# A ring of thirteen parts for gathered rows, walked in steps of two parts in place of five

## The chip, the cores and the metric

The kernel runs on one core of a Trainium2 chip, from one launch. The metric is the device time of the program in microseconds (us); lower is better. The unchanged kernel was run three times: 1429.01, 1425.98 and 1428.95 us, median 1428.95. Its engines are PE (TensorE), DVE (VectorE), ACT (ScalarE), POOL (GpSimd) and SP (SyncE); each works through its own instructions in program order and they meet by semaphores.

## What is computed

One decoder layer over 512 tokens of width 1024, all float32. A mixing part (causal stick-breaking attention with 8 heads of 64, beside a chunked gMLP, and one output projection) gives x1 by a layer norm. Then comes the part that takes most of the time, a retrieval of experts by product keys, cut from the reference:

```
q = (x @ w_q).reshape(B, S, 8, 2, 128)                  # 8 retrieval heads
scores = einsum('bshpk,hpnk->bshpn', q, sub_keys)       # two halves, 128 keys each
s1, i1 = top_k(scores[..., 0, :], 16);  s2, i2 = top_k(scores[..., 1, :], 16)
top_s, top_c = top_k(s1[..., :, None] + s2[..., None, :], 16)
ids = i1[top_c // 16] * 128 + i2[top_c % 16]            # 16 experts for each token and head
gates = softmax(top_s)
h   = einsum('thkd,td->thk', u_tab[ids], x)             # a dot with a row of u for each expert
act = gates * gelu(h)
out = einsum('thk,thkd->td', act, v_tab[ids])           # a weighted sum of the rows of v
```

So for each of 512 tokens, 8 heads and 16 experts a row of u (4 KB) and a row of v (4 KB) are needed. Afterwards a layer norm, a sigmoid gate with a per-layer embedding and a last layer norm follow.

## The kernel before, in words

**Units and rows.** Tokens lie on the 128 partitions, in four tiles. A unit is one tile with one head; there are 32 (`UNITS`), numbered from 0 in the order in which they are worked. A unit has 16 columns c, one for each chosen expert, and a column is one *row* here: one indirect DMA that brings, for each of the 128 tokens, the 8 KB row of the joined table `uv` (1024 floats of u, then 1024 of v), 1 MiB in all. The rows are numbered k = 16 u + c, 0 to 511.

**What is done with a row.** POOL issues the gather (L652). DVE forms the dot of its u half with x1 (L1813, a multiply with a running sum, written back into the same place; a short instruction then reads the sum into `hid`). ACT takes the gelu of a pair of columns at once (L1429), multiplies by the gates (L1432) and scales the v halves of both rows in place (L1439). PE adds each scaled row into PSUM by eight 128x128 transposes (L1181, `combine`), which count `slot_free` up by one for a row.

**The ring.** The rows live in `ring`, the first 14 x 1024 floats of each partition of `arena`: thirteen parts of 1024 floats and one spare behind, so that a row that begins at part 12 has room. A row takes two neighbouring parts, u half and v half. Row k begins at part (3 + 5k) mod 13. So the part of its u half is next written as the v half of row k + 5, and that of its v half as the u half of row k + 8. This is what the two waits ahead of each gather say: row k waits for the dot of row k - 5 (L646, `dots_done`, `U_LIFE`) and for the sum of row k - 8 (L648, `slot_free`, `V_LIFE`). The landings of the rows are told by eight semaphores `rows_in` in turn, and DVE waits for the one of its row (L1811).

```
part = (FIRST_PART + U_LIFE * (u * TOPK + c)) % PARTS
return ring[:, part * D:(part + 2) * D]
```

**The order of the work.** It is written out by hand. POOL has nothing but the gathers from 73 us on: a unit's gathers wait besides for its `ids`. DVE's stream is two dots, then a piece of other work, and so on: the ranking of the next unit's keys (`rank_keys`, `rank_sums`, `rank_rest`, `rank_ids`), the norms and other pieces of the tiles that are behind (`background`), and `add_run`, which takes a finished sum from PSUM. ACT has a pair of columns, then its background work, and once in each unit, at the column pair 5, the exponentials of the next unit's gates between two loads of function tables (L1477, L1485). PE has the transposes of each row; after those of column 10 the 32 matmuls of `query(u + 2)` (L866), after those of column 12 the four of `key_scores(u + 2)` (L878), and after each odd column a step of background matmuls (the projections of the other tiles, attention, output and gate products). Four queries stand elsewhere (`EARLY`). SP issues the weight loads.

```
for c in range(TOPK):
    combine(u, c)
    if c == 10 and u + 2 < NU and u + 2 not in EARLY:
        query(u + 2)
    if c == 12 and u + 2 < NU:
        key_scores(u + 2)
```

**The start and the end.** Before the gathers the ring holds other things: `w_out0` in parts 0 to 7, `e_0`, `l_0`, `pre_T` and `pre_q` in parts 8 and 9, and the first weights `w_gv` of the gv projection in parts 10, 11 and half of 12. Therefore two gathers of unit 0 wait for these projections (`gv_halves`, L642 and L644): column 4, which begins at part 10, and column 7, at part 12. In the last unit the columns from 11 on are gathered without the last quarter of their v half, two of them without any of it, and these pieces follow in seven gathers after row 511 (L660, L666).

Of the kernel before, what the change touches and what calls it, by code (L numbers as in the profile page):

```python
# [24 lines left out]
PH, TOPK, NKEY = 8, 16, 128  # L25
# [6 lines left out]
MASKED = -float(2 ** 30)  # L32
SEED = 1597463007.0

U_LIFE, V_LIFE = 5, 8
PARTS = U_LIFE + V_LIFE
FIRST_PART = 3
GRP = 2
OUT_PIECES = ((0, 512), (512, 832), (832, 1024))
LAST_COLS = (0, 288, 576, 864, D)  # L40
# [143 lines left out]
def build(nc, a, out):  # L184
    ctx = ExitStack()
    with ctx:
# [3 lines left out]
        def sem(name):  # L190
            return ctx.enter_context(nc.semaphore(name))
# [70 lines left out]

        def row(u, c):

            part = (FIRST_PART + U_LIFE * (u * TOPK + c)) % PARTS
            return ring[:, part * D:(part + 2) * D]

        late_sum = row(NU - 1, LATE)[:, PART:2 * D]
        y_1 = row(NU - 1, LATE)[:, 0:HALF]


# [109 lines left out]
        gv_halves = sem("gv_halves")  # L381
# [51 lines left out]
        rows_in = [sem(f"rows_in{i}") for i in range(V_LIFE)]  # L433
# [172 lines left out]
        @block.gpsimd  # L606
        def _(pool):
            nc.gpsimd.memset(ident[:, :], 0.0).then_inc(const_ready, 1)
            nc.gpsimd.memset(neg_tri[:, :], -1.0).then_inc(const_ready, 1)
            nc.gpsimd.memset(neg_one[:, :], -1.0).then_inc(const_ready, 1)  # L610
            nc.gpsimd.memset(neg_mask[:, :], MASKED).then_inc(const_ready, 1)
            nc.gpsimd.memset(ones[:, :], 1.0).then_inc(const_ready, 1)
            nc.gpsimd.iota(iota16[:, :], pattern=[[1, TOPK]], base=0, channel_multiplier=0,
                           allow_small_or_imprecise_dtypes=True).then_inc(const_ready, 1)
            pool.wait_ge(const_ready, 6)
            nc.gpsimd.affine_select(out=ident[:, :], in_=ident[:, :], compare_op=ALU.not_equal, fill=1.0,
                                    base=0, pattern=[[-1, P]], channel_multiplier=1).then_inc(const_ready, 1)
            nc.gpsimd.affine_select(out=neg_tri[:, :], in_=neg_tri[:, :], compare_op=ALU.is_ge, fill=0.0,
                                    base=0, pattern=[[-1, P]], channel_multiplier=1).then_inc(const_ready, 1)
            nc.gpsimd.affine_select(out=neg_mask[:, :], in_=neg_mask[:, :], compare_op=ALU.is_ge, fill=0.0,  # L620
                                    base=0, pattern=[[-1, P]], channel_multiplier=1).then_inc(const_ready, 1)
            pool.wait_ge(ws_in, 16)
            nc.gpsimd.affine_select(out=wsT, in_=wsT, compare_op=ALU.is_ge, fill=0.0, base=0,
                                    pattern=[[0, G], [1, P]], channel_multiplier=-1).then_inc(ws_masked, 1)


            for buf, ready, done in ((l_0, l_ready, l_masked), (e_0, a_ready, a_masked)):
                pool.wait_ge(ready, 1)
                blk = buf.rearrange("p i (h n) -> p (i h) n", n=P)
                nc.gpsimd.affine_select(out=blk, in_=blk, compare_op=ALU.is_gt, fill=0.0, base=0,  # L630
                                        pattern=[[0, AH], [1, P]], channel_multiplier=-1).then_inc(done, 1)

            def gather_unit(u):
                if u:
                    pool.wait_ge(ids_ready, u + 3)
                for c in range(TOPK):
                    if u == 0 and c in (0, 1, TOPK // 2):
                        pool.wait_ge(ids_ready, (0, 1, TOPK // 2).index(c) + 1)
                    if u == 0 and c == 0:
                        pool.wait_ge(score_done, 1)  # L640
                    if u == 0 and c == 4:
                        pool.wait_ge(gv_halves, 1)  # L642
                    if u == 0 and c == 7:
                        pool.wait_ge(gv_halves, 2)  # L644
                    if u * TOPK + c >= U_LIFE:
                        pool.wait_ge(dots_done, u * TOPK + c - U_LIFE + 1)  # L646
                    if u * TOPK + c >= V_LIFE:
                        pool.wait_ge(slot_free, u * TOPK + c - V_LIFE + 1)  # L648
                    n = PART if u == NU - 1 and c >= LATE else 2 * D
                    if u == NU - 1 and c >= TOPK - 2:  # L650
                        n = D
                    nc.gpsimd.indirect_dma_start(  # L652
                        out=row(u, c)[:, 0:n], out_offset=None, in_=a["uv"][:, :],
                        in_offset=bass.IndirectOffsetOnAxis(ap=ids[:, u % 4, c:c + 1], axis=0),
                    ).then_inc(rows_in[c % V_LIFE], 16)

            for u in range(NU):
                gather_unit(u)
            for c in range(TOPK - 2, TOPK):
                nc.gpsimd.indirect_dma_start(  # L660
                    out=row(NU - 1, c)[:, D:PART], out_offset=None, in_=a["uv"][:, :],
                    in_offset=bass.IndirectOffsetOnAxis(ap=ids[:, (NU - 1) % 4, c:c + 1], axis=0),
                    element_offset=D,
                ).then_inc(values_in[c - TOPK + 2], 16)
            for c in range(LATE, TOPK):
                nc.gpsimd.indirect_dma_start(  # L666
                    out=row(NU - 1, c)[:, PART:2 * D], out_offset=None, in_=a["uv"][:, :],
                    in_offset=bass.IndirectOffsetOnAxis(ap=ids[:, (NU - 1) % 4, c:c + 1], axis=0),
                    element_offset=PART,
                ).then_inc(late_in[c - LATE], 16)  # L670
# [846 lines left out]
        def _(dve):  # L1517
# [287 lines left out]
            def dots(u, g):  # L1805
                i, t = u % 4, UNITS[u][0]
                if u == 0 and g == 0:
                    dve.wait_ge(x1_ready, 2)
                for c in range(g * GRP, (g + 1) * GRP):
                    r = row(u, c)[:, 0:D]  # L1810
                    dve.wait_ge(rows_in[c % V_LIFE], u * (16 * TOPK // V_LIFE) + 16 * (c // V_LIFE + 1))  # L1811
                    r = r.rearrange("p (k n) -> p k n", k=KD)
                    v.tensor_tensor_reduce(out=r, in0=r, in1=x1[t], scale=1.0, scalar=0.0,  # L1813
                                           op0=ALU.mult, op1=ALU.add,
                                           accum_out=hid[:, i, c:c + 1]).then_inc(dots_done, 1)
# [194 lines left out]
            for u in range(NU):  # L2010
                for g in range(NG):
                    if u == 1 and g == 0:
                        norm_gates(1)
                    dots(u, g)
                    if u == 0 and g == 0:
                        norm_gates(0)
                    if u and RUN[u] != RUN[u - 1] and g == (0 if RUN[u] < 3 else 1 if RUN_END[RUN[u - 1]] in (21, 26) else 5):
                        add_run(RUN[u - 1])
                    if u + 1 < NU:
                        first = 0 if u else 2  # L2020
                        if g in (first, first + 1):
                            rank_keys(u + 1, g - first)
                        if g == (first + 2 if u else 3):
                            rank_sums(u + 1)
                        if g == (first + 3 if u else 4):
                            rank_rest(u + 1)
                        if g == (first + 4 if u else 5):
                            rank_ids(u + 1)
                    if 0 < u < NU - 1 and g == 6:
                        norm_gates(u + 1)  # L2030
                    background(u * NG + g)
# [3 lines left out]
            c, i = TOPK - 1, (NU - 1) % 4  # L2035
# [88 lines left out]
```

## Time and profile before

| what | value |
|---|---|
| median of the runs | 1428.95 us |
| profiled execution | 1429.69 us, of which the span is 1427.9 us |
| busy share of the span | PE 79%, DVE 76%, ACT 66%, POOL 39% |
| chain that ended last, by engine | DMA 48%, PE 21%, DVE 16%, issue 7%, ACT 5%, POOL 2% |
| packets | 584.06 MB, mean 409 GB/s |
| gathers | 512 of the rows (L652) and 7 pieces at the end |

All times come from one profiled execution, in us from the start of its span. A line of a timeline gives the start, the duration, the engine, the line of the kernel, the instruction, what it writes and reads, how many instructions were merged into the line (x16), and in brackets the idle time of the engine before it with what ended it. PEclk is the granted share of PE's full clock. A wait for two semaphores is put down to the event that came last by the trace.

### The profile page before, as it was taken

How to read it: one execution, taken by the hardware profiler on the slowest of the kernel's cores; microseconds unless marked ns; L12 is line 12 of the kernel's file. 1: busy time of each engine (PE TensorE's matmuls, PEld its weight loads, DVE VectorE, ACT ScalarE, POOL GpSimd, SP SyncE). 2: the span in 40 equal slices, each digit the busy share in tenths (PEclk: the TensorE clock that was granted, in tenths of full speed). 3: DMA queues.
4: the chain of work that ended last, by engine and by line, in shares of the span. 5: the costliest groups of instructions: out<-in, count | busy, mean ns of one | idle time of the engine just before them, and what ended most of it. 6: DMA issues, size and time to landing. Idle time of an engine off the chain costs nothing.

```text
span 1427.9 us, 19363 instructions
## 1 busy us (share of the span) xinstructions
PE 1130.4 (79%) x6804; PEld 878.7 (62%) x6804; DVE 1078.6 (76%) x2602; ACT 937.0 (66%) x1613; POOL 563.4 (39%) x535
## 2 busy tenths in 40 slices
PE   9999999988679877688646987877668776777656
PEld 4567777666677666576546556656556665555545
DVE  1488776768878886778757668977887788878768
ACT  2246678579878888766636666657666766667563
POOL 1044444334544444444324334434434434433342
PEclk9999999999999999998878989889778888878988
DMA  9799999999999999999999999999999999999994
GB/s 357 275 390 426 423 426 392 425 416 426 414 424 407 425 426 426 426 426 420 426 429 426 425 425 406 424 384 425 425 427 415 424 427 426 427 427 426 426 425 162
DMA packets 89787, 584.06 MB, mean 409 GB/s; under 512 B 9709, under 2 KB 15253, under 8 KB 22490
## 3 DMA queue, kind: packets, MB, share of 16 engines
q0 software_dynamic: 74288, 536.90, 90.0%
q1 hardware_dynamic: 15402, 45.92, 8.2%
q8 instruction: 53, 0.87, 0.2%
q14 instruction: 44, 0.36, 0.1%
HBM read 580.69 MB, written 2.10 MB: 408 GB/s over the span
## 4 chain that ended last, share of the span: by engine, by line
DMA 48%; PE 21%; DVE 16%; issue 7%; ACT 5%; POOL 2%; POOLq 0%; DVEq 0%; ACTq 0%
DMA arena<-in_uv,ids 48%; DVE arena L1813 9%; PE ps L1181 6%; ACT arena L1439 2%; PE ps L866 2%; PE ps L1000 2%; PE ps L1076 2%; POOL arena L652 2%; PE ps L696 1%; PE ps L686 1%; PE ps L679 1%; ACT actv L1432 1%; PE ps L943 0%; PE ps L936 0%; PE ps L763 0%
## 5 line engine op out<-in xcount | busy, mean ns | idle before, releaser
L652 POOL DMA_INDIRECT arena<-in_uv,ids x512 | 550.3, 1075 | 805.0 <-DVE hid L1813 545.1
L1181 PE MATMUL ps<-ident,arena 128*128 128x128 f32 x4076 | 607.5, 307 | 279.5 <-ACT arena L1439 278.0
L1181 PEld LDWEIGHTS ps<-ident,arena 128*128 128x128 f32 x4076 | 528.7, 158 | 379.3 <-ACT arena L1439 337.9
L1813 DVE CUSTOM_DVE_ANT_1 arena<-arena 128x1024 f32<-128x1024 f32 x384 | 468.3, 1225 | 196.1 <-DMA arena<-in_uv,ids 185.1
L1439 ACT ACTIVATE arena<-arena,actv 128x1024 f32<-128x1024 f32 x511 | 554.2, 1131 | 0.2
L1429 ACT ACTIVATE gel<-hid 128x2 f32<-128x2 f32 (+1 forms) x257 | 52.1, 203 | 379.1 <-DVE hid L1813 376.5
L1813 DVE CUSTOM_DVE_ANT_0 arena<-arena 128x1024 f32<-128x1024 f32 x128 | 155.7, 1225 | 65.7 <-DMA arena<-in_uv,ids 64.8
L1432 ACT ACTIVATE actv<-gel,gates 128x1 f32<-128x1 f32 x511 | 122.9, 287 | 8.4
L866 PE MATMUL ps<-arena 128*128 128x128 f32 x992 | 122.7, 285 | 0.0
L866 PEld LDWEIGHTS ps<-arena 128*128 128x128 f32 x992 | 120.6, 202 | 0.0
L1000 PE MATMUL ps<-arena 128*128 128x384 f32 x192 | 65.9, 486 | 0.0
L1076 PE MATMUL ps<-arena 128*128 128x512 f32 (+2 forms) x160 | 60.2, 523 | 0.0
L1485 ACT ACT_TABLE_LOAD x45 | 57.7, 1283 | 0.8
L1477 ACT ACT_TABLE_LOAD x45 | 57.7, 1283 | 0.8
L831 PE MATMUL ps<-arena 128*128 128x512 f32 x96 | 45.1, 615 | 2.5 <-DVE arena L1823 2.1
L1000 PEld LDWEIGHTS ps<-arena 128*128 128x128 f32 x192 | 34.6, 190 | 19.1
L1076 PEld LDWEIGHTS ps<-arena 128*128 128x128 f32 x160 | 29.5, 198 | 21.1 <-issue 18.9
L1813 DVE DVE_READ_ACCUMULATOR2_ANT hid<- 128x1 f32 x512 | 42.1, 82 | 0.0
L831 PEld LDWEIGHTS ps<-arena 128*128 128x128 f32 x96 | 18.2, 199 | 21.5 <-issue 18.3
L686 PE MATMUL ps<-arena 128*128 128x512 f32 x64 | 29.1, 597 | 0.7 <-ACT arena L1339 0.7
L679 PE MATMUL ps<-arena 128*128 128x512 f32 x64 | 28.9, 594 | 0.0
L1682 DVE TENSOR_TENSOR cands<-cands,topf 128x512 f32<-128x512 f32 x31 | 21.5, 692 | 1.1
(268 smaller groups left out, 1004.5 us busy)
## 6 DMA issues: line engine op xcount, KB each, us to landing
arena<-in_wq SPq DMA_DIRECT2D x10, 1024.0 KB, 9.6
arena<-in_uv,ids POOLq DMA_INDIRECT x519, 5.1
arena<-in_w_out SPq DMA_DIRECT2D x2, 2048.0 KB, 12.5
arena<-in_w_gate SPq DMA_DIRECT2D x1, 4096.0 KB, 16.6
arena<-in_w_out SPq DMA_DIRECT2D x3, 1024.0 KB, 13.5
arena<-in_w_k SPq DMA_DIRECT2D x4, 512.0 KB, 7.3
arena<-in_w_q SPq DMA_DIRECT2D x2, 1024.0 KB, 10.3
arena<-in_w_v SPq DMA_DIRECT2D x2, 1024.0 KB, 10.8
```

Of the source, the lines that this page charges most:

```text
L652: nc.gpsimd.indirect_dma_start(out=row(u, c)[:, 0:n], out_offset=None, in_=a["uv"][:, :], in_offset=bass.IndirectOffsetOnAxis(ap=ids[:, u ...
L831: i = mm(ps[:, bank, :], src[:, c, :], w[:, c, j * HALF:(j + 1) * HALF], start=(c == 0), stop=(c == WB - 1))
L866: i = mm(ps[:, 7, half * P:(half + 1) * P], wq[b][k][:, half * P:(half + 1) * P], x1T[t][:, k, :], start=(k == 0), stop=(k == KD - 1))
L1000: i = mm(ps[:, piece_bank(p), 0:REST], w[:, b * D + k * P:b * D + (k + 1) * P], xT[:, k, :], start=(k == 0), stop=(k == KD - 1), skip_grou ...
L1076: m = mm(ps[:, bank, place:place + c1 - c0], acc[t][:, k * P:(k + 1) * P], w_gate[:, k, c0:c1], start=(k == 0 and place == 0), stop=(k == ...
L1181: i = mm(ps[:, run_bank(r) + k // 4, (k % 4) * P:(k % 4 + 1) * P], row(u, c)[:, D + k * P:D + (k + 1) * P], ident[:, :], is_transpose=True ...
L1429: fn(gel[:, i, cols], hid[:, i, cols], ACT.Gelu).then_inc(gel_ready, 1)
L1432: fn(actv[:, i, c:c + 1], gel[:, i, c:c + 1], ACT.Copy, scale=gates[:, i, c:c + 1])\
L1439: fn(r, r, ACT.Copy, scale=actv[:, i, c:c + 1]).then_inc(scaled, 1)
L1477: act.preload_act_table_set("natural_log_exp_and_others")
L1485: act.preload_act_table_set("gelu_and_others")
L1813: v.tensor_tensor_reduce(out=r, in0=r, in1=x1[t], scale=1.0, scalar=0.0, op0=ALU.mult, op1=ALU.add, accum_out=hid[:, i, c:c + 1]).then_inc ...
```

## The change

The step of the ring becomes two parts: row k begins at part 2k mod 13. The part of its u half is then next written as the v half of row k + 6 (12 is 13 less one), and that of its v half as the u half of row k + 7 (14 is 13 and one). So row k waits for the dot of row k - 6 and the sum of row k - 7. The landing semaphores are seven, counted through over all rows. In unit 0 the parts 10 to 13 are first met by columns 5 and 6, and these wait for the gv projections.

```diff
--- before.py
+++ after.py
@@ -32,9 +32,9 @@
 MASKED = -float(2 ** 30)
 SEED = 1597463007.0
 
-U_LIFE, V_LIFE = 5, 8
+U_LIFE, V_LIFE, NEXT_ROW = 6, 7, 2
 PARTS = U_LIFE + V_LIFE
-FIRST_PART = 3
+assert U_LIFE * NEXT_ROW % PARTS == PARTS - 1 and V_LIFE * NEXT_ROW % PARTS == 1
 GRP = 2
 OUT_PIECES = ((0, 512), (512, 832), (832, 1024))
 LAST_COLS = (0, 288, 576, 864, D)
@@ -262,7 +262,7 @@
 
         def row(u, c):
 
-            part = (FIRST_PART + U_LIFE * (u * TOPK + c)) % PARTS
+            part = NEXT_ROW * (u * TOPK + c) % PARTS
             return ring[:, part * D:(part + 2) * D]
 
         late_sum = row(NU - 1, LATE)[:, PART:2 * D]
@@ -638,10 +638,8 @@
                         pool.wait_ge(ids_ready, (0, 1, TOPK // 2).index(c) + 1)
                     if u == 0 and c == 0:
                         pool.wait_ge(score_done, 1)
-                    if u == 0 and c == 4:
-                        pool.wait_ge(gv_halves, 1)
-                    if u == 0 and c == 7:
-                        pool.wait_ge(gv_halves, 2)
+                    if u == 0 and c in (5, 6):
+                        pool.wait_ge(gv_halves, c - 4)
                     if u * TOPK + c >= U_LIFE:
                         pool.wait_ge(dots_done, u * TOPK + c - U_LIFE + 1)
                     if u * TOPK + c >= V_LIFE:
@@ -652,7 +650,7 @@
                     nc.gpsimd.indirect_dma_start(
                         out=row(u, c)[:, 0:n], out_offset=None, in_=a["uv"][:, :],
                         in_offset=bass.IndirectOffsetOnAxis(ap=ids[:, u % 4, c:c + 1], axis=0),
-                    ).then_inc(rows_in[c % V_LIFE], 16)
+                    ).then_inc(rows_in[(u * TOPK + c) % V_LIFE], 16)
 
             for u in range(NU):
                 gather_unit(u)
@@ -1808,7 +1806,7 @@
                     dve.wait_ge(x1_ready, 2)
                 for c in range(g * GRP, (g + 1) * GRP):
                     r = row(u, c)[:, 0:D]
-                    dve.wait_ge(rows_in[c % V_LIFE], u * (16 * TOPK // V_LIFE) + 16 * (c // V_LIFE + 1))
+                    dve.wait_ge(rows_in[(u * TOPK + c) % V_LIFE], 16 * ((u * TOPK + c) // V_LIFE + 1))
                     r = r.rearrange("p (k n) -> p k n", k=KD)
                     v.tensor_tensor_reduce(out=r, in0=r, in1=x1[t], scale=1.0, scalar=0.0,
                                            op0=ALU.mult, op1=ALU.add,
```

## Rows read from the trace of the kernel before

**Rows 1.** The page: rate in 40 slices of the span; the gathers' queue.

```profile
GB/s 357 275 390 426 423 426 392 425 416 426 414 424 407 425 426 426 426 426 420 426 429 426 425 425 406 424 384 425 425 427 415 424 427 426 427 427 426 426 425 162
...
q0 software_dynamic: 74288, 536.90, 90.0%
```

**Rows 2.** Busy time by stretch: window, engines' busy time, clock, DMA share, GB/s.

```profile
80.00:1400.00 1320.00, 1033.71 (x6448) 824.65 (x6447) 1025.84 (x2451) 909.99 (x1567) 551.18 (x512) 0.89 1.01 421
920.00:940.00 20.00, 17.25 (x122) 14.53 (x121) 15.99 (x46) 13.91 (x25) 7.26 (x7) 0.96 0.91 358
```

**Rows 3.** Waits of POOL: in total, times, longest.

```profile
POOL arena L652 <- DVE hid L1813: 545.1, 319, 11.2
POOL arena L652 <- PE ps L1181: 180.1, 93, 4.2
```

**Rows 4.** Timeline of a steady stretch, rows 196, 197, 201 among others.

```profile
600.78 1.21 DVE L1813 CUSTOM_DVE_ANT_1 arena<-arena 128x1024 f32<-128x1024 f32 x1
...
602.26 0.94 POOL L652 DMA_INDIRECT arena<-in_uv,ids  x1 [0.95 <-DVE hid L1813]
...
602.83 1.23 DVE L1813 CUSTOM_DVE_ANT_1 arena<-arena 128x1024 f32<-128x1024 f32 x1 [0.84 <-DMA arena<-in_uv,ids]
...
605.91 2.13 PE L1181 MATMUL ps<-ident,arena 128*128 128x128 f32 x16 [1.43 <-ACT arena L1439]
...
612.56 1.23 DVE L1813 CUSTOM_DVE_ANT_1 arena<-arena 128x1024 f32<-128x1024 f32 x1 [0.31 <-DMA arena<-in_uv,ids]
```

**Rows 5.** Timeline of the deepest dip: gathers and dots of rows 323, 325.

```profile
926.92 0.94 POOL L652 DMA_INDIRECT arena<-in_uv,ids  x1 [3.51 <-DVE hid L1813]
...
934.93 1.23 DVE L1813 CUSTOM_DVE_ANT_1 arena<-arena 128x1024 f32<-128x1024 f32 x1 [0.80 <-DMA arena<-in_uv,ids]
935.12 1.84 POOL L652 DMA_INDIRECT arena<-in_uv,ids  x1 [2.96 <-PE ps L1181]
...
941.55 1.23 DVE L1813 CUSTOM_DVE_ANT_1 arena<-arena 128x1024 f32<-128x1024 f32 x1 [2.66 <-DMA arena<-in_uv,ids]
```

**Rows 6.** Timeline at column 11 of unit 0 and of unit 29.

```profile
109.95 1.22 DVE L1813 CUSTOM_DVE_ANT_0 arena<-arena 128x1024 f32<-128x1024 f32 x1 [0.40 <-DMA arena<-in_uv,ids]
...
119.12 1.04 PE L1181 MATMUL ps<-ident,arena 128*128 128x128 f32 x8
...
120.93 1.01 POOL L652 DMA_INDIRECT arena<-in_uv,ids  x1 [2.85 <-PE ps L1181]
...
1314.69 1.25 DVE L1813 CUSTOM_DVE_ANT_1 arena<-arena 128x1024 f32<-128x1024 f32 x1 [0.28 <-DMA arena<-in_uv,ids]
...
1322.67 2.04 PE L1181 MATMUL ps<-ident,arena 128*128 128x128 f32 x16
```

**Rows 7.** Timeline at column 11 of unit 15, row 251.

```profile
747.79 1.28 DVE L1813 CUSTOM_DVE_ANT_1 arena<-arena 128x1024 f32<-128x1024 f32 x1 [0.25 <-DMA arena<-in_uv,ids]
...
752.69 4.47 PE L866 MATMUL ps<-arena 128*128 128x128 f32 x32
...
755.17 0.94 POOL L652 DMA_INDIRECT arena<-in_uv,ids  x1 [2.49 <-DVE hid L1813]
...
757.00 1.91 PE L1181 MATMUL ps<-ident,arena 128*128 128x128 f32 x16
...
758.81 1.77 POOL L652 DMA_INDIRECT arena<-in_uv,ids  x1 [2.70 <-PE ps L1181]
```

**Rows 8.** Timeline, dots and transposes of rows 80 and 462.

```profile
303.90 1.23 DVE L1813 CUSTOM_DVE_ANT_0 arena<-arena 128x1024 f32<-128x1024 f32 x1 [0.39 <-DMA arena<-in_uv,ids]
...
312.52 3.96 PE L1181 MATMUL ps<-ident,arena 128*128 128x128 f32 x32
...
1282.81 1.22 DVE L1813 CUSTOM_DVE_ANT_1 arena<-arena 128x1024 f32<-128x1024 f32 x1 [0.86 <-DMA arena<-in_uv,ids]
...
1291.18 4.18 PE L1181 MATMUL ps<-ident,arena 128*128 128x128 f32 x32
```

**Rows 9.** Timeline of POOL at the start, column 7 of unit 0.

```profile
87.95 1.45 POOL L652 DMA_INDIRECT arena<-in_uv,ids  x1 [0.30 <-issue]
```

## The prediction

> **What bounds the kernel now.** I read the page first. One gathered row is 1 MiB, 512 of them are 536.9 MB, and their queue takes 90.0% of the transfer engines' time; from the fourth of the 40 slices to the last but one the rate stands near 426 GB/s, with a few dips [rows 1]; the chain that ended last runs over those gathers more than over any engine. So the end is set by how steadily rows are transferred: one takes 536.9 MB / 512 / 426 GB/s = 2.46 us. Then the window from 80 to 1400 us, in which all 512 gathers start: 421 GB/s [rows 2], so what is lost there to dips is (426 - 421) / 426 x 1320 = 15.5 us. That is all that any ring can win in the middle.
>
> Then the waits of POOL, which issues the gathers: 319 ended with a dot (545.1 us), 93 with a sum on PE (180.1 us) [rows 3]. That reads as a ring short of dot slots. It isn't a loss by itself: a gather that starts late still finds older rows in the queue. What counts is how long a gather may be held back before the engines run dry, and which of the two events comes last after the change.
>
> **The budget of the ring.** Row numbers count the gathers from 0, sixteen to a unit. In a steady stretch the gather at 602.26 is row 201 and its dot starts at 612.56, released by the DMA: 10.3 us [rows 4]. In the worst dip, 358 GB/s over 920 to 940 us [rows 2], the gather at 926.92 landed for the dot at 934.93, after 8.0 us, and the one at 935.12 for the dot at 941.55, after 6.4 us [rows 5]. At 8.0 the engines begin to stand idle, at 6.4 they had stood empty; the truth for "begins to cost" lies between 6.4 and about 9.6 (10.3 less a part of the 2.46 us of one queued row). I take 8.0, the row nearest to the start of a dip, and keep the ends.
>
> A row's second part comes free when its sum is done. From a gather to the gather that reuses that part go: 8.0 us to the dot's start, 1.24 us of dot (1.22 to 1.23 in the rows), the lag from the dot's end to the end of the row's transposes, and 0.77 us from there to the gather (sum ending at 119.12 + 1.04 = 120.16, gather at 120.93 [rows 6]). With eight rows of 2.46 us this fits if the lag is at most 19.7 - 10.0 = 9.65 us; with seven, 17.2 - 10.0 = **7.2 us**. The dot's part needs 8.0 + 1.24 + 0.27 = 9.5 us (0.27: dot of row 196 over by 601.99, gather at 602.26 [rows 4]) of 12.3 now and 14.8 after. So the dots had 2.8 us to spare and get 2.5 more that nothing needs, and the sums lose 2.46 us.
>
> **What it removes.** The wait for dot k-5 becomes k-6: worth at most the dips that a dot ended. I take a third, 5 us, of the 15.5: most of POOL's waits end with a dot [rows 3], but in the deepest dip the gather at 935.12 had waited 2.96 us for PE [rows 5], and such a dip is not won. Bounds 0 and 15.5.
>
> **What it adds.** The wait for sum k-8 becomes k-7. In a steady stretch the lag is 604.06 to 608.04 = 4.0 us for the odd row of a pair (dot at 602.83 + 1.23, sixteen transposes from 605.91 for 2.13) and about 5 to 5.5 for the even one, whose scaling waits for its partner's dot [rows 4]: under 7.2, cost nothing. Their cover is the queue, 10.3 - 8.0 = 2.3 us of it; if it is gone, they cost too (rival 4).
>
> It is otherwise at column 11 of every unit. There PE runs the 32 matmuls of a query between the transposes of column 10 and those of column 11. In unit 15: dot of row 251 from 747.79, over at 749.08; query from 752.69 for 4.47; then the transposes of rows 251 and 252 from 757.00, the first eight over near 757.95: lag 8.9 us, and column 3 of the next unit, eight rows later, started at 758.81, by PE's release [rows 7]. After the change column 2, which went out at 755.17, waits for that same sum: 3.6 us later, of which the queue hides 2 or so. The price by the budget is 8.9 - 7.2 = 1.7 us. The same reading of all 30 units that have a successor gives lags from 4.2 to 11.5; the first is unit 0 (dot 109.95 + 1.23, sum 120.16: 9.0) and the last unit 29 (dot over at 1315.95, first eight of the transposes from 1322.67 over near 1323.7: 7.8) [rows 6]. In 26 of them the lag or that of a neighbour passes 7.2, and the excess over 7.2, less what passed 9.65 already, adds to **35 us**. Outside column 11 there are 17 stretches in which background matmuls do the same; the first is at row 80 (dot over at 305.13, the first eight of the transposes from 312.52 near 313.6: lag 8.4) and the last at row 462 (dot over at 1284.03, first eight of those from 1291.18 near 1292.2: 8.2) [rows 8]: together **17 us**. One such stretch costs once, since what it holds back shifts every later event alike.
>
> **Moved at no cost.** At the start the wait for the projections of gv moves from columns 4 and 7 to 5 and 6, as parts 10 to 12 are now met there; column 4 goes out earlier, column 7 waits for sum 0, which the gather at 87.95 [rows 9] didn't: two us or so at most, under the queue's 2.3; were it bare, it would cost those two us once. Seven landing semaphores in place of eight hold the seven rows that can be in flight. Same 512 + 7 gathers, same bytes, same dots and transposes, no instruction added on ACT, DVE or PE; SP's queue is untouched. The last unit's late halves lie in other parts but keep their order. ACT and PE work behind a late row is not lengthened, but PE idles more and its clock, 0.89 over the window [rows 2], may fall: 0 to 5 us, inside the range.
>
> **Sum.** 35 + 17 - 5 = +47. The profiled execution took 1429.69 (span 1427.9 and 1.8 around it), 0.74 above the median of 1428.95; so 1476.7 by it and **1476 us** by the median. With 6.4 us as the point of loss the limit for the lag is 8.8, the two groups shrink to 16 and 6, and the sum is +17; with 9.6 the limit is 5.6 and they grow to 58 and 30: +83.
>
> The Trainium skill, page "DMA: Bandwidth & Descriptors", section "Anatomy of one DMA — SWDGE (gpsimd) path", gives a gather's time as about 2.0 us plus bytes / 436 GB/s, which is 4.4 us for a row. By it the limit for the lag would be 17.2 - 4.4 - 2.0 = 10.8 us, and the sum close to nothing. The shortest of this trace's rows, 6.4 us with the engines dry, speaks against it.
>
> **Rivals.** A measurement of this kernel tells about 0.2% (2.9 us) from no change.
> 1. Faster. POOL waits three times as long for dots as for sums [rows 3]; if the dips belong to the dots (a dot late by over 2.8 us behind DVE's other work) and the sums catch up while the feed is slower, the sixth dot slot fills dips: up to 15.5 us, 1413. It decides from the point where sum k-7 frees its part before dot k-5 would: two rows less the difference of 0.77 and 0.27, so for lags under 4.9 - 0.5 = 4.4 us, which odd rows have and even ones don't. Against it: column 3 is released by PE in both units shown [rows 6, 7]. 5%.
> 2. The queue is deeper than I read, so that lags up to 9 us are hidden: 1429 to 1432. Against: the 6.4 and 8.0 us of [rows 5]. 5%. (The page named above would give this one.)
> 3. Only an empty queue costs: +17, 1446. For it: in the deepest dip the engines still moved 84% of the full rate. 13%.
> 4. The ring becomes the bound everywhere: lags of 5.5 pass the limit of 5.6 as soon as PE's clock or the landing is a little worse. +83, 1512. Against: at 8.0 an ordinary row still has 1.7 us. 12%.
> The forecast has 65%. Range: leaving out rivals 1 and 2, and half of each of 3 and 4, 1448 to 1504, both inside the ends of +17 and +83. Slower 0.90, same 0.05, faster 0.05.
>
> **What would show it.** POOL's waits turn round: most end with PE, few with a dot. In a new profile the rate has a dip near column 2 of nearly each unit, the window's mean falls to about 407 GB/s (421 x 1320 / 1367), the gather of column 2 starts 0.77 us after the sum of column 11, bytes and counts stay. Wrong would be: waits for PE but no dips (rival 2), a steady row period over 2.46 us between dips (rival 4), or dots still ending most waits (rival 1).

## The result and the profile after

The changed kernel takes 1461.41 us (median of 4 runs, 1459.28 to 1466.3) against 1428.98 us for the kernel before (4 runs): a ratio of 1.0224 with a 95% interval of 1.0207 to 1.0241, or 32 us more. Its profiled execution took 1461.42 us, with a span of 1459.7 us.

The page of the changed kernel, for [rows 1]: the rate in 40 slices, the gathers' queue and the chain that ended last, by engine.

```profile
GB/s 352 265 381 425 389 388 384 425 421 423 381 425 393 413 411 403 426 410 412 421 419 410 409 425 410 414 405 417 410 427 391 413 426 402 423 426 426 426 426 152
...
q0 software_dynamic: 74288, 536.90, 89.3%
...
DMA 40%; PE 28%; DVE 14%; ACT 11%; issue 6%; POOL 1%; POOLq 0%; DVEq 0%
```

The bytes are the same, to the packet. The rate isn't: where before most slices stood at 424 to 427, now slices of 381 to 415 are spread over the whole middle. The share of DMA in the chain fell from 48 to 40%, and PE and ACT took it: the chain now often runs through the way from a dot to its sum.

The table of busy time by stretch, for [rows 2] (window, busy time of PE, PEld, DVE, ACT and POOL, clock, DMA share, GB/s), here over 80 to 1432 us:

```profile
80.00:1432.00 1352.00, 1044.65 (x6462) 834.64 (x6461) 1030.10 (x2460) 912.99 (x1571) 596.60 (x516) 0.88 1.00 412
```

421 GB/s over 1320 us became 412 over 1352, the same product within 0.3%. PE, DVE and ACT are as busy in sum as they were, within 1.1% (POOL is up from 551 to 597 us, as each gather instruction takes longer); the whole difference is idle transfer time. The waits of POOL, for [rows 3]:

```profile
POOL arena L650 <- PE ps L1179: 433.0, 174, 7.0
POOL arena L650 <- DVE hid L1811: 226.2, 100, 5.1
POOL arena L650 <- issue: 89.4, 233, 4.2
```

They turned round: by these lines PE ends 174 waits in place of 93, a dot 100 in place of 319. The lines name the event that came last, not the one that the gather needed. The times of the instructions are sharper: a held gather starts 0.77 us after the end of the sum that it waits for, or 0.28 us after the end of its dot. Counted within 0.1 us over rows 16 to 511:

| kernel | dot, sum, rows back | gathers released by their sum | by their dot |
|---|---|---|---|
| before | 5, 8 | 79 | 311 |
| changed | 6, 7 | 315 | 2 |
| experiment 1 | 5, 7 | 278 | 56 |
| experiment 2 | 7, 7 | 310 | 0 |

So in the changed kernel the dots release next to nothing. And the head of unit 16, for [rows 7]:

```profile
770.06 1.23 DVE L1811 CUSTOM_DVE_ANT_1 arena<-arena 128x1024 f32<-128x1024 f32 x1 [1.66 <-DMA arena<-in_uv,ids]
...
774.07 3.74 PE L864 MATMUL ps<-arena 128*128 128x128 f32 x32
...
777.64 1.04 PE L1179 MATMUL ps<-ident,arena 128*128 128x128 f32 x8
778.97 1.09 PE L1179 MATMUL ps<-ident,arena 128*128 128x128 f32 x8 [0.29 <-ACT arena L1437]
779.45 0.94 POOL L650 DMA_INDIRECT arena<-in_uv,ids  x1 [2.50 <-PE ps L1179]
...
780.84 0.99 POOL L650 DMA_INDIRECT arena<-in_uv,ids  x1 [0.45 <-issue]
```

Row 251 is column 11 of unit 15: its dot is over at 771.29, the query's 32 matmuls follow, and its own eight transposes end at 778.68. The gather of column 2 of the next unit starts 0.77 us later, at 779.45, released by PE: what column 3 did before. The sum of column 12 is done at 780.06, and column 3 goes out 0.78 us behind it, at 780.84, though its line says `issue`.

Where this hurts shows at the head of unit 24 (the gathers of columns 1, 2 and 3 and the dots of columns 2 and 3):

```profile
1107.82 0.94 POOL L650 DMA_INDIRECT arena<-in_uv,ids  x1 [3.65 <-PE ps L1179]
...
1112.26 0.94 POOL L650 DMA_INDIRECT arena<-in_uv,ids  x1 [3.51 <-DVE hid L1811]
...
1116.57 1.19 POOL L650 DMA_INDIRECT arena<-in_uv,ids  x1 [3.37 <-PE ps L1179]
...
1119.79 1.22 DVE L1811 CUSTOM_DVE_ANT_1 arena<-arena 128x1024 f32<-128x1024 f32 x1
...
1122.40 1.23 DVE L1811 CUSTOM_DVE_ANT_1 arena<-arena 128x1024 f32<-128x1024 f32 x1 [1.39 <-DMA arena<-in_uv,ids]
```

Three gathers in a row go out 4.4 and 4.3 us apart, where a row is transferred in 2.46. All three follow a sum: the one at 1112.26 too, whose line names a dot. Its own dot was over at 1104.67, and its sum (column 11 of unit 23) ended at 1111.49, 0.77 us before it. The last, of 1116.57, is there for its dot at 1122.40, after 5.8 us in place of the usual 10. Only the row before it was still on its way, and the transfer engines ran out of work before this row's packets began, as the DMA share and the rate show (last two columns; window, busy time of PE, PEld, DVE, ACT and POOL, clock before them):

```profile
1116.00:1117.00 1.00, 1.00 (x12) 1.00 (x11) 1.00 (x3) 0.01 (x1) 0.43 (x1) 1.00 0.95 401
1117.00:1118.00 1.00, 1.00 (x12) 1.00 (x10) 0.93 (x6) 0.97 (x4) 0.76 (x1) 1.00 0.20 82
```

To place the loss I took from both traces, for each row, when the first of its sixteen partial landings is recorded, and compared the steps from row to row, summed by column. From row 16 to row 506 the stream became 28 us longer: 22 of these at the columns 1 to 5 (+2.1, +15.8 at column 2, +12.0 at column 3, -1.5, -6.5), 6 at all others, most of it at columns 11 and 13. The rest of the 32 us lies at the start and the end. Some 2 us of it are no effect of the change: the first gather started at 75.4 in place of 73.5 us, and of the variants below one with the start of before had 75.4 (experiment 1), one with the changed start 73.5 (experiment 3).

### The profile page after: what moved, and what is told of

It is laid out like the page before. It is cut to its first block, busy times and chain, and to the rows that moved or that the text cites. A ratio compares the mean times of both kernels' runs of the same rounds, so it can differ in the third digit from the quotient of the medians.

```text
span 1459.7 us, 19364 instructions
## 1 busy us (share of the span) xinstructions
PE 1142.0 (78%) x6804; PEld 889.6 (61%) x6804; DVE 1079.0 (74%) x2602; ACT 937.4 (64%) x1613; POOL 606.3 (42%) x535
## 4 chain that ended last, share of the span: by engine, by line
DMA 40%; PE 28%; DVE 14%; ACT 11%; issue 6%; POOL 1%; POOLq 0%; DVEq 0%
DMA arena<-in_uv,ids 40%; PE ps L1179 10%; DVE arena L1811 8%; ACT arena L1437 4%; PE ps L1074 3%; PE ps L998 2%; PE ps L684 2%; PE ps L864 2%; ACT actv L1430 2%; PE ps L694 1%; PE ps L677 1%; ACT L1475 1%; ACT L1483 1%; POOL arena L650 1%; ACT gel L1427 1%
## 5 line engine op out<-in xcount | busy, mean ns | idle before, releaser
L650 POOL DMA_INDIRECT arena<-in_uv,ids x512 | 593.7, 1160 | 790.0 <-PE ps L1179 433.0
L1179 PE MATMUL ps<-ident,arena 128*128 128x128 f32 x4076 | 623.1, 312 | 299.5 <-ACT arena L1437 298.1
L1179 PEld LDWEIGHTS ps<-ident,arena 128*128 128x128 f32 x4076 | 541.1, 161 | 402.6 <-ACT arena L1437 365.9
L1680 DVE TENSOR_TENSOR cands<-cands,topf 128x512 f32<-128x512 f32 x31 | 21.5, 693 | 1.1
```

The costliest lines, as they stand in the source:

```text
L650: nc.gpsimd.indirect_dma_start(out=row(u, c)[:, 0:n], out_offset=None, in_=a["uv"][:, :], in_offset=bass.IndirectOffsetOnAxis(ap=ids[:, u ...
L1179: i = mm(ps[:, run_bank(r) + k // 4, (k % 4) * P:(k % 4 + 1) * P], row(u, c)[:, D + k * P:D + (k + 1) * P], ident[:, :], is_transpose=True ...
```

## The experiments

All ratios are to the kernel before, on the same chip, with 95% intervals. A ratio can differ a little from the quotient of the two medians, most in experiment 6 (1.0223 against 1.0198). The diffs are cut to the lines that matter; `...` stands for what is left out.

**1. The sum wait alone, in the old ring.**

```diff
-                        pool.wait_ge(slot_free, u * TOPK + c - V_LIFE + 1)
+                        pool.wait_ge(slot_free, u * TOPK + c - V_LIFE + 2)
```

> The ring of before (steps of five parts, dot five rows back, eight landing semaphores, the old places and start), with the wait for the sum seven rows back in place of eight. Theory (the sums' slot is what costs): as slow as the changed kernel, 1.020 to 1.026 of before, 1457 to 1466 us. Rival A (the places of the parts, the seven semaphores or the moved waits at the start cost): little here, under 1.008. Rival B (the sixth dot slot won something back in the changed kernel): slower than the changed kernel by what it won, 1.03 or more.

Measured: 1465.71 us, 1.0245 (1.0208 to 1.0283). All of the slowdown is there with the old places, the old start and eight semaphores: rival A falls. The waits of POOL in it:

```profile
POOL arena L652 <- PE ps L1181: 376.9, 155, 6.2
POOL arena L652 <- DVE hid L1813: 304.7, 147, 10.1
```

**2. A looser dot wait.** The same fourteen parts as seven pairs:

```diff
-U_LIFE, V_LIFE, NEXT_ROW = 6, 7, 2
-PARTS = U_LIFE + V_LIFE
+U_LIFE, V_LIFE, NEXT_ROW = 7, 7, 2
+PARTS = 14
...
-        ring = take((PARTS + 1) * D)
+        ring = take(PARTS * D)
```

> The same fourteen parts used as seven fixed pairs: a row waits for the dot and the sum of the row seven back. Against the changed kernel only the dot wait is looser (seven for six). Theory: the dot wait no longer decides, so the same as the changed kernel within 3 us, 1.020 to 1.025 of before. Rival B (dots still end dips in the changed kernel): faster than it by 5 us or more.

Measured: 1462.81 us, 1.0249 (1.0216 to 1.0281). With 1 that brackets the changed kernel: dots five, six or seven back are the same to within the intervals as long as the sum is seven back. Rival B falls. In the trace of 2 the lines give PE 169 of POOL's waits, and by the times no gather was released by its dot.

**3 and 4. The query in two halves**, in the changed kernel and in the kernel before:

```diff
-                    if c == 10 and u + 2 < NU and u + 2 not in EARLY:
-                        query(u + 2)
+                    if c in (10, 11) and u + 2 < NU and u + 2 not in EARLY:
+                        query(u + 2, (c - 10,))
```

(`query` takes the halves to compute as a second argument.)

> The changed kernel with the query's 32 matmuls cut into two halves of 16, the first after the transposes of column 10, the second after those of column 11. Theory (late sums at column 11 are two thirds of the cost): the sum of column 11 comes nearly 2 us earlier where PE was busy, and 8 to 20 us of the 32 come back, 1.009 to 1.017 of before. Rival C (the ring is slow everywhere, not at columns): less than 4 us come back.

> The kernel before with the same cut of the query. Theory: with eight rows for the sums only lags over 9.65 us cost, so 0 to 5 us are won, 0.996 to 1.000. Rival C: the same gain or none in both kernels. If the cut itself is good for PE whatever the ring, the gain is as large as in the changed kernel.

Measured: 1458.18 us, 1.0223 (1.0198 to 1.0248), and 1428.17 us, 1.0000 (0.9988 to 1.0012). In the changed kernel I had expected 8 to 20 us back; the medians are 3 us apart, which can't be told from no change. The head of unit 16 in its trace says why:

```profile
773.00 1.95 PE L864 MATMUL ps<-arena 128*128 128x128 f32 x16
...
774.79 1.04 PE L1180 MATMUL ps<-ident,arena 128*128 128x128 f32 x8
...
775.66 1.95 PE L864 MATMUL ps<-arena 128*128 128x128 f32 x16
776.60 0.94 POOL L650 DMA_INDIRECT arena<-in_uv,ids  x1 [1.72 <-PE ps L1180]
...
777.90 1.09 PE L1180 MATMUL ps<-ident,arena 128*128 128x128 f32 x8 [0.29 <-ACT arena L1438]
...
779.77 1.37 POOL L650 DMA_INDIRECT arena<-in_uv,ids  x1 [2.23 <-PE ps L1180]
```

The sum of column 11 ends at 775.83, 5.6 us after its dot in place of 7.4, and column 2 goes out earlier. But the sum of column 12 ends at 778.99 and column 3 waits for it: the late sum was only handed to the next row. By column the loss at 2 fell from 15.8 to 6.3 us, while at 3 it was 13.8 for 12.0.

**5 and 6. Without the table loads.** ACT loads two tables around the exponentials of each unit's gates, between the pairs of columns 10 and 12, and I suspected these. A gelu, for which the table is in place, stands for the exponential, so these kernels compute other gates:

```diff
-                fn(expv[:, i, :], best[:, i, :], ACT.Exp, bias=negmax[:, i:i + 1],
+                fn(expv[:, i, :], best[:, i, :], ACT.Gelu if u else ACT.Exp, bias=negmax[:, i:i + 1],
...
-                if logs or exps or ranked:
+                if logs or exps:
```

> The changed kernel without the two table loads around the exponentials of each unit's gates; a gelu, whose table is in place, stands for the exponential, so the gates are other numbers and everything else is as large as before. The cut of the query alone took the loss from column 2 and left that at column 3 (13.8 us of the stream in its trace), which waits for the sum of column 12. Theory D (that sum is late since ACT spends 3 us on loads and exponentials between the pairs of columns 10 and 12): without the loads the sum of column 12 comes up to 2.6 us earlier, but column 2 still waits for the query, so 4 to 12 us come back, 1.014 to 1.020. Rival (PE alone makes the sums late, by the query and the four score matmuls): under 3 us come back.

> Both at once: no table loads around the gates' exponentials (a gelu in their place, other gates) and the query in two halves. Theory D: neither column 2 nor 3 finds a late sum, and most of the loss of columns 1 to 5 (22 us of the stream) comes back, 1.005 to 1.012 of before. Rival (a ring of seven is too short even for ordinary lags of 5.5 us): more than 20 us of the 32 stay, 1.014 or more.

Measured: 1464.58 us, 1.0248 (1.0228 to 1.0267), where 4 to 12 us were expected back, and with the cut of the query besides 1457.59 us, 1.0223 (1.0183 to 1.0263), where most of 22 us were. Theory D falls: 25 of the 45 pairs of loads are gone, at 1.28 us a load 64 us of ACT's time (the 20 pairs left belong to units whose attention needs them), and nothing clear of the noise comes back. The rival that I had set beside the second, a ring too short even for ordinary lags, is not refuted by this.

**7. One dot slot less, in the old ring.**

```diff
-                        pool.wait_ge(dots_done, u * TOPK + c - U_LIFE + 1)
+                        pool.wait_ge(dots_done, u * TOPK + c - U_LIFE + 2)
```

> The kernel before with the wait for the dot four rows back in place of five; the sum stays eight back. By the budget of the prediction a dot's part needs about 9.5 us, and four rows give 9.8: the other side of the exchange is nearly used up too. Theory: dots that start late behind DVE's other work now cost, 1.006 to 1.025. If dots have as much room as the change assumes none need: 1.000 to 1.003.

Measured: 1489.84 us, 1.0437 (1.0414 to 1.0461): 61 us, well past the 36 us at the top of what I expected. POOL's waits in it:

```profile
POOL arena L652 <- DVE hid L1813: 621.7, 350, 9.5
POOL arena L652 <- PE ps L1181: 153.4, 80, 5.4
```

**8. The exchange the other way**, four rows for the dot and nine for the sum:

```diff
-U_LIFE, V_LIFE, NEXT_ROW = 6, 7, 2
+U_LIFE, V_LIFE, NEXT_ROW = 4, 9, 3
...
-                    if u == 0 and c in (5, 6):
-                        pool.wait_ge(gv_halves, c - 4)
+                    if u == 0 and c in (3, 4):
+                        pool.wait_ge(gv_halves, c - 2)
```

(The landing semaphores are eight again.)

> The exchange turned the other way: thirteen parts in steps of three, so that a row waits for the dot four rows back and the sum nine back; eight landing semaphores. Theory (five and eight lie near the best split of thirteen): slower than before by what the fourth dot slot costs less at most 5 us for the ninth sum slot, 1.003 to 1.022. If the sums are the only limit of the ring: faster than before, 0.991 to 0.998.

Measured: 1483.61 us, 1.0383 (1.0349 to 1.0417), beyond the 1.022 at the top of what I expected, since giving up the fifth dot slot cost more than I had put it at. Against 7 the ninth sum slot gives back some 6 us, at the edge of the intervals; giving up the fifth dot slot costs 61. Five and eight is the best of the three splits of thirteen that were run.

**9 and 10. The query earlier.** The halves after columns 7 and 9:

```diff
-                    if c == 10 and u + 2 < NU and u + 2 not in EARLY:
-                        query(u + 2)
+                    if u + 2 < NU and u + 2 not in EARLY:
+                        if any(kept_early(u, e) for e in range(TOPK)):
+                            if c == 10:
+                                query(u + 2)
+                        elif c in (7, 9):
+                            query(u + 2, ((c - 7) // 2,))
```

> The changed kernel with the query's two halves after the transposes of columns 7 and 9 in place of 10 (in the four units that have an early query besides it stays whole at column 10). The cut at 10 and 11 left the PE work between the sums of columns 10 and 12 as long as it was, which is why the sum of column 12, and with it the gather of column 3, stayed late. Theory E (what costs is PE's work ahead of the sums of columns 11 and 12, as the ring of seven has about 1 us of room over an ordinary lag): columns 2 and 3 lose little, of the 28 us of the stream 10 to 20 come back, some given away again at columns 15 and 1; 1.007 to 1.016 of before. Rival (something else at the head of a unit holds columns 2 and 3, the ids or DVE's ranking): they lose as much as before, 1.020 or more.

> The kernel before with the same earlier halves. Theory E: its ring of eight hides these lags but for the worst units, so 0 to 6 us are won, 0.996 to 1.000. If it is as much as in the changed kernel (10 us or more), the early place is good in itself and says nothing of the ring.

Measured: 1484.21 us, 1.0382 (1.0352 to 1.0411), and 1448.02 us, 1.0129 (1.0111 to 1.0147). Both are slower, where a gain or nothing was expected, and by another thing than the one under test: in three units the query came ahead of what it reads. PE in the changed kernel's variant:

```profile
347.51 3.78 PE L864 MATMUL ps<-arena 128*128 128x128 f32 x16 [5.64 <-DMA arena<-in_wq]
...
395.84 1.41 PE L864 MATMUL ps<-arena 128*128 128x128 f32 x5 [4.49 <-ACT arena L1337]
```

In unit 5 PE waited for the query's weights. In unit 6, and again in unit 10 (3.1 us at 568.29), it waited for ACT's copy of the next tile's transposed x1 (L1337), while the weights were there: in unit 6 since 347.5.

By unit the loss of this variant to the kernel before is largest in these units, 5, 6 and 10 (10.1, 6.4 and 8.8 us). In the units from 12 on, which hold none, the stream of this variant lost 11.9 us to the kernel before and that of the changed kernel 12.2: no gain to be seen there either. As a test of theory E the pair is inconclusive; both rings lose about 20 us with such waits in place.

**11 and 12. ACT takes each column by itself.** The first row of a pair no longer waits for its partner's dot:

```diff
-                    activate_rows(u, slice(g * GRP, (g + 1) * GRP - ends), u * NG + g + 1 + ends)
...
+                for c in range(g * GRP, (g + 1) * GRP):
+                    if u * TOPK + c + 1 < NU * TOPK:
+                        activate_rows(u, slice(c, c + 1), u * TOPK + c + 1)
```

> The changed kernel with ACT taking each column by itself, as its dot is there, in place of two columns at once: one more gelu per pair on ACT, and the first row of a pair no longer waits for its partner's dot. That wait is in every even row's lag (5.5 us against 4.0 of the odd ones). Theory F (a ring of seven has hardly any room over the ordinary even lag, and what PE adds at columns 11 and 12 comes on top): even lags fall by 1 to 1.5 us, column 12's too, and 10 to 22 us of the 32 come back, 1.007 to 1.016 of before. Rival (only PE's background work makes sums late, whatever ACT does): the sums of columns 11 and 12 end at the same times and under 5 us come back, 1.019 or more.

> The kernel before with the same single columns on ACT. Theory F: dots end its waits, and only a few units have sums late enough for a ring of eight, so 0 to 6 us are won, 0.996 to 1.000. If ACT's extra work (some 256 gelus of 0.2 us and their waits) makes the sums later at its busy places: slower, 1.001 to 1.006.

Measured: 1444.10 us, 1.0093 (1.0073 to 1.0113), and 1428.75 us, 0.9988 (0.9976 to 1.0000). Here the slowdown goes from 2.24 to 0.93%, 19 us back in the changed kernel and 0 to 3 in the one before, whose ring had the room. The single columns at the head of unit 16:

```profile
760.26 1.23 DVE L1808 CUSTOM_DVE_ANT_1 arena<-arena 128x1024 f32<-128x1024 f32 x1 [0.36 <-DMA arena<-in_uv,ids]
...
762.62 3.74 PE L864 MATMUL ps<-arena 128*128 128x128 f32 x32
...
766.19 1.04 PE L1179 MATMUL ps<-ident,arena 128*128 128x128 f32 x8
...
768.00 1.59 POOL L650 DMA_INDIRECT arena<-in_uv,ids  x1 [3.22 <-PE ps L1179]
```

The query starts as soon as the sum of column 10 is done, and that is now earlier: 2.4 us after the dot of column 11 began, against 4.0 (774.07 - 770.06) in the changed kernel; the sum of column 11 ends at 767.23, 5.7 us after its dot in place of 7.4. Over rows 16 to 499 the lag from dot to sum fell from 5.95 to 4.76 us in the mean, and the loss at columns 1 to 5 from 22 to 7 us. So a shorter way from dot to sum is worth 19 us in the ring of seven and next to nothing in the ring of eight. At which rows it counts isn't separated by this run, since the lag fell everywhere: at column 11 from 7.84 to 6.51 us in the mean, at column 12 from 7.65 to 6.55, at the columns outside 10 to 13 from 5.63 to 4.41. Experiment 6 speaks for the ordinary rows having a part: there the lags were 6.25 and 7.09 at columns 11 and 12 and still 5.65 elsewhere, and at most 4 us came back.

## Why the prediction was right, point by point

**The direction and its cause** are shown. The sum slot costs (1), the dot slots beyond the fifth give nothing (1 and 2), the gathers are released by sums in place of dots (315 to 2), columns 2 and 3 carry most of the loss, and column 2 starts 0.77 us after the sum of column 11. The measured 1461.41 us lies in the range of 1448 to 1504, half way between rival 3 (1446) and the forecast of 1476; the size alone doesn't choose between the two.

**The size** was 47 us by the sum and is 32. The terms of 35 (column 11) and 17 (elsewhere) were mis-sized: the stream shows 22 and 6. Two steps stand behind them, and the runs don't say how much each was off. One is the landing time below which a late gather costs, taken as 8.0 us. In the changed kernel's trace the 24 rows that landed under 7.5 us after their gather began took 21.5 us in all beyond their 2.46 each, the 33 at 7.5 to 8.0 took 5.5, and the 31 at 8.0 to 8.5 took 8.1. That suggests that most of the price is paid below 7.5, but counted by the last partial landing in place of the first the three groups took 8.9, 8.6 and 7.7 us, so no point at which the price begins can be read from it. The other step is the count of the late sums. With 7.0 us in place of 8.0 the limit of the lag becomes 8.2, and the prediction's count gives 21 + 8 = 29 us, close to the 28 found; but that is a fit after the fact, and the count itself has a gap. It begins its 17 stretches at row 80. In rows 1 to 66 of the kernel before, five more pass the limit, with lags of 9.9 to 11.9 us (row 52: dot over at 217.95, sum at 229.90); at the prediction's price, 2.46 us each at most, they would have added 12 us, and the forecast would have been 1488; the fit with 7.0 would miss by nearly as much. That the forecast came as near as it did is in part luck. Before the change some dips sat at column 5, and the 6.5 us that this column lost less seem to have moved to columns 2 and 3 instead of being added; the prediction had no term for it.

**The dots' gain** of 5 us isn't there. 1 and 2 differ by two dot slots and not in time. The rule by which I gave it, a share of the dips, had no mechanism behind it. In the kernel before 311 gathers were released by their dot and the stream still ran near its full rate; in the changed kernel two were, and the extra slot had nothing to give.

**The dots' room** was wrong in the other direction, without harm to this forecast. I read 2.8 us to spare with five slots (12.3 less 9.5), hence 0.3 with four; 7 shows 61 us. The budget left out that a landed row often waits for DVE, which is argued here and not tested by a run of its own: in the trace of 7 the even columns' dots start 0.2 to 1.2 us after the landing in the mean. To keep the pace with four slots a row may land at most 9.84 - 1.24 - 0.27 = 8.3 us after its gather, less that wait, where they landed after 8.8 us in the mean, so nearly every row is at the edge.

**The place of the cause** I had as PE's query at column 11. The late sum there is in the trace, but moving half of the query away gave nothing: 3 took the delay from column 11 and lost it again at column 12; 5 and 6 removed ACT's loads and got nothing. What came back came with a shorter lag at all rows (11). The prediction said that an ordinary row, 4.0 us for an odd one and 5 to 5.5 for an even one, was under the limit and cost nothing. Those rows were at the low end: over the trace of the kernel before, rows 16 to 499 with columns 10 to 13 left out, the lag is 5.69 us in the mean, odd rows among them at 5.3 rather than 4.0. That these lags use up the room that the busy columns need fits 6 and 11, and isn't shown by itself.

**The rivals.** Rival 1 (faster by dots) and the places and semaphores are excluded by 1 and 2. Rival 2 (a deep queue) is excluded by the result. Rival 3 (only an empty queue costs) is not: the measured time lies as near to it as to the forecast, and the engines did run empty at the head of unit 24. The page "DMA: Bandwidth & Descriptors" of the Trainium skill, section "Anatomy of one DMA — SWDGE (gpsimd) path", would give 4.4 us for a row, as an estimate; the gather at 1116.57, before whose packets the engines had run dry, took 5.8 us to its dot, so the measurement decides against using that figure for this gather. Rival 4 (the ring as the bound at every row) is excluded by slices that still stand at 425 to 427 GB/s.

**A slip:** the prediction has all 512 gathers start between 80 and 1400 us; four of them start before 80, which changes nothing in its sum.

**Open:** why 5.8 us pass from a gather to its landing though the engines have run dry, where the price of a late gather begins, whether the lag at ordinary rows or that at columns 11 and 12 is the one that 11 shortened with effect, and what part of the loss outside columns 1 to 5 belongs to which background work. Whether an early query with its weights and its x1 there in time would help wasn't tried.

## What to carry to other kernels

In a ring that two consumers free in turn, who ends most waits doesn't tell which slot is worth more: before the change 311 gathers were released by dots while little was lost, and one more dot slot gave nothing. Nor does the name in a wait's line tell who released it; compare the start with the end of the very event that it waits for. Write down for each slot the full way round (issue to landing with a nearly empty queue, the wait for the engine, the work, the way to the second consumer, release), compare with slots times the row's transfer time, and move a slot only from a consumer with room. Where the room is small, shorten the way at all rows first (19 us here); moving one late piece of work handed the delay to the next row.

## What the runs showed of the hardware

A 1 MiB gather of 128 rows of 8 KB landed after about 10.3 us behind a full queue, and after 5.8 us where only the row before was still on its way and the engines ran dry (the gather at 1116.57); no row between 16 and 506 of the two traces landed sooner than 5.7 us after its gather. The gather instruction itself took longer in the changed kernel, 1160 ns in the mean against 1075 before, though its form is the same; why stays open. The first gather started at 73.5 us in some executions and at 75.4 in others of equal code up to there, so 2 us of a single profile's difference can come from the start.
